# First block's mixer: band matmuls for the pooled means, token-major HGRN output, full-width projection chunks

## The reference

```python
u_pool, q_pre, f_pre, i_in, og, gates = split(h @ w_in)      # 512, 512, 512, 512, 512, 2048 columns
# pool branch: 4 groups of 128 columns, windows 2, 4, 8, 16
pooled[t] = mean of u_pool over the last min(t+1, w) tokens
pool_out  = ((pooled - u_pool) @ pool_w[group]) * pool_scale
# HGRN branch: 4 heads of 128; f_pre gives a decay per token, k = (1-lb)*sigmoid(-f_pre), q = silu(q_pre)
o = hgrn2_chunkwise(q, k, v=i_in, log_f)                     # decayed causal linear attention
o = o * rsqrt(mean(o*o over the head's 128 columns) + 1e-6) * hgrn_norm
hgrn_out = o * silu(og)
merged = sigmoid(g0) * (pool_out @ w_pool_proj) + sigmoid(g1) * (hgrn_out @ w_hgrn_proj)
return merged @ w_out
```

## Time and profile before

| | |
|---|---|
| median of 3 runs | 2721.94 us |
| the profiled execution | 2722.93 us, span 2720.9 us, mean granted TensorE clock 0.974 |
| busy in the span | TensorE 95%, VectorE 57%, ScalarE 46%, GpSimd 4% |
| DMA | 453.30 MB, 167 GB/s on average |
| first mixer call | z chunks start at 228.60 us, w_out goes on at 388.69 us |
| second mixer call | z chunks start at 807.11 us, w_out goes on at 975.98 us |

### The profile page before, as it was taken

One profiled execution on the slowest core, in us unless ns is written; L12 is line 12 of the kernel. 1 busy time (PEld: TensorE's weight loads), 2 busy tenths in 40 slices (PEclk: granted clock), 3 DMA queues, 4 the chain that ended last, 5 costly groups with the idle time before them and its releaser, 6 DMA issues.

```text
span 2720.9 us, 33264 instructions
## 1 busy us (share of the span) xinstructions
PE 2572.2 (95%) x14040; PEld 2216.7 (81%) x14040; DVE 1541.2 (57%) x1557; ACT 1246.6 (46%) x1336; POOL 100.3 (4%) x154
## 2 busy tenths in 40 slices
PE   7999889999998889999998899899999998999998
PEld 6889878888888878887888788788888887798787
DVE  5556855555467765464556436655554665365654
ACT  4436534434446444444443665444343434744442
POOL 0001300000001200000000010000000000100000
PEclk9999989999999999999999899999999988999999
DMA  7545135455443345465543225454554432253552
GB/s 271 186 163 208 68 133 212 172 203 201 170 174 140 109 143 213 170 230 184 197 180 117 87 103 206 153 210 170 190 211 174 178 131 93 98 197 139 203 180 96
DMA packets 69571, 453.30 MB, mean 167 GB/s; under 512 B 7808, under 2 KB 9984, under 8 KB 19632
## 3 DMA queue, kind: packets, MB, share of 16 engines
q1 hardware_dynamic: 64080, 432.22, 43.9%
...
## 4 chain that ended last, share of the span: by engine, by line
PE 82%; DVE 8%; ACT 6%; issue 4%; DMA 0%; POOL 0%; DVEq 0%; SPq 0%; ACTq 0%; POOLq 0%
PE acc L508 20%; PE acc L510 20%; PE acc L509 20%; PE acc L476 5%; PE acc L478 5%; PE acc L477 5%; ACT w_hi L409 3%; DVE w_lo L413 2%; PE aux L577 1%; PE aux L670 0%; PE stat L524 0%; PE bc L524 0%; DMA raw<-in_w 0%; PE aux L944 0%; DVE tmp L1624 0%
## 5 line engine op out<-in xcount | busy, mean ns | idle before, releaser
L413 DVE TENSOR_TENSOR w_lo<-raw,w_hi 128x2048 fp32r<-128x2048 f32 (+1 forms) x438 | 944.6, 2159 | 827.0 <-ACT w_hi L409 825.0
L409 ACT ACTIVATE w_hi<-raw 128x2048 fp32r<-128x2048 f32 (+1 forms) x438 | 787.6, 1802 | 657.4 <-PE acc L510 580.1
L508 PE MATMUL acc<-w_hi,x_hi 128*128 128x512 f32 (+1 forms) x1632 | 641.6, 393 | 31.3 <-DVE x_lo L1699 19.7
L510 PE MATMUL acc<-w_lo,x_hi 128*128 128x512 f32 (+1 forms) x1632 | 635.2, 389 | 0.0
L509 PE MATMUL acc<-w_hi,x_lo 128*128 128x512 f32 (+1 forms) x1632 | 634.9, 389 | 0.0
L508 PEld LDWEIGHTS acc<-w_hi,x_hi 128*128 128x128 f32 x1632 | 308.9, 189 | 98.6 <-issue 25.2
L476 PE MATMUL acc<-x_hi,w_hi 128*128 128x256 f32 x1280 | 371.2, 290 | 5.3 <-DVE w_lo L413 5.3
L477 PE MATMUL acc<-x_lo,w_hi 128*128 128x256 f32 x1280 | 366.2, 286 | 0.0
L478 PE MATMUL acc<-x_hi,w_lo 128*128 128x256 f32 x1280 | 366.0, 286 | 0.0
L510 PEld LDWEIGHTS acc<-w_lo,x_hi 128*128 128x128 f32 x1632 | 308.6, 189 | 63.9
L509 PEld LDWEIGHTS acc<-w_hi,x_lo 128*128 128x128 f32 x1632 | 308.9, 189 | 61.2
...
## 6 DMA issues: line engine op xcount, KB each, us to landing
...
```

What stands on the lines that cost most here:

```text
L409: nc.scalar.activation(w_hi[:, slot, 0:kind], raw[:, slot, 0:kind], ACT.Copy).then_inc(hi_done, 1)
L413: nc.vector.tensor_tensor(w_lo[:, slot, 0:kind], raw[:, slot, 0:kind], w_hi[:, slot, 0:kind].bitcast(F32), ALU.subtract).then_inc(lo_done, 1)
L508: nc.tensor.matmul(out, vh, wh, start=first and k == 0, stop=False)
L510: last = nc.tensor.matmul(out, vh, wl, start=False, stop=last_k and k == nk - 1)
```

## The change

- **Pooled means.** u is no longer transposed and summed. TensorE multiplies the token-major u by a constant band matrix per group, which gives (mean - u) channel-major in one step: 144 columns from the first 128 tokens, 128 from the second. ScalarE copies the result out, and the pool matrices follow one chunk later. GpSimd's sums and VectorE's block of means are gone; the constants (`mixc`, 128 x 1600) are loaded on GpSimd's queue behind `pool_w`.
- **Forget gates.** ScalarE and VectorE do each step for both halves of z before the next step, behind the splits of chunks 8 and 9.
- **Order of the units.** Unit 0 waits for k and q only. The nine iterations now run with chunks 8 to 16 (output gate twice, token-major over both chunks; then seven gate chunks), and chunk 17 follows unit 17. Two output-gate steps of VectorE stand in iteration 1, the pool branch's low parts in iteration 2.
- **HGRN output.** It is computed token-major. ScalarE squares each head with the sum as a second output and takes the root, VectorE multiplies by inverse root and output gate in one step, TensorE transposes the product, and ScalarE and VectorE split it. Statistics matmuls and broadcast are gone.
- **Projections.** Their weights come as four wide chunks instead of eight half ones (26 chunks per mixer instead of 30). `proj` runs half a chunk into one bank, so the order of the matmuls stays.
- **Merge.** VectorE has one split between the four merge steps instead of one behind each.

```diff
-MIX1 = [WIDE] * 18 + [HALF] * 8 + [WIDE] * 4
+MIX1 = [WIDE] * 26
...
+def mixer_constants(i):
+
+
+    s, t = np.arange(2 * P)[:, None], np.arange(2 * P)[None, :]
+    bands = []
+    for w in WINDOWS:
+        m = ((s <= t) & (s > t - w)) / np.minimum(t + 1, w) - (s == t)
+        bands += [m[:P, :BAND], m[P:, P:]]
+    bands = np.concatenate(bands, 1).astype(np.float32)
+    gain = [np.broadcast_to(i["hgrn_norm"][l], (P, 512)) for l in range(LAYERS)]
+    return np.ascontiguousarray(np.stack([np.concatenate([bands, g], 1) for g in gain]))
...
-                turn_block(UT, lambda p: pe.wait_ge(u_rows, 2 * (l + 1)), l, u_turned)
-                for j in range(5, 10):
+                pe.wait_ge(mixc_loaded, 16 * (l + 1))
+                pe.wait_ge(u_rows, 2 * (l + 1))
+                for g in range(4):
+                    band, cols = MIXC[:, g * BANDS:(g + 1) * BANDS], slice(g * P, (g + 1) * P)
+                    out = flips[g // 2][:, (g % 2) * S:(g % 2 + 1) * S]
+                    nc.tensor.matmul(out[:, 0:BAND], UT[:, 0, cols], band[:, 0:BAND], start=True, stop=False,
+                                     skip_group_check=True)
+                    last = nc.tensor.matmul(out[:, P:S], UT[:, 1, cols], band[:, BAND:BANDS], start=False, stop=True,
+                                            skip_group_check=True)
+                    if g % 2:
+                        last.then_inc(pooled_done, 1)
+                two_tiles(c0 + 5, t0 + 5, 8, x_hi, x_lo)
+                for g in range(4):
+                    if g % 2 == 0:
+                        pe.wait_ge(pooled_ready, 2 * l + g // 2 + 1)
+                    last = nc.tensor.matmul(flips[g // 2][:, (g % 2) * S:(g % 2 + 1) * S], pool_w[:, g * P:(g + 1) * P],
+                                            PD[:, g], start=True, stop=True)
+                    if g % 2:
+                        last.then_inc(pool_mixed, 1)
+                for j in range(6, 8):
...
-                            pe.wait_ge(forget_ready, 1 + 2 * l + 1)
-                            pe.wait_ge(pool_parts, 4 * (l + 1))
+                            pe.wait_ge(k_ready, 2 * (l + 1))
+                            pe.wait_ge(q_ready, 2 * (l + 1))
...
+                def proj(c, tile, a, src_hi, src_lo, wait_k):
+
+                    if a == 0:
+                        chunk_ready(c)
+                    bank_free(tile)
+                    for tl in range(2):
+                        for k in range(4):
+                            if tl == 0 and a == 0:
+                                wait_k(k)
+                            last = mm3(ps(tile)[:, tl * S:(tl + 1) * S], *wblock(c % RING, 8 * a + 4 * tl + k),
+                                       src_hi[:, k], src_lo[:, k], k == 0, k == 3)
+                    last.then_inc(chunk_done if a else tile_done, 1)
...
+                for j in range(9):
+                    if j < 2:
+                        both(c0 + 8 + j, t0 + 8, j)
+                    else:
+                        two_tiles(c0 + 8 + j, t0 + 8 + j, 8, x_hi, x_lo)
                     unit(2 * j)
                     unit(2 * j + 1)
-                unit(16)
-                unit(17)
-                two_tiles(c0 + 18, t0 + 18, 4, br_hi, br_lo)
+                two_tiles(c0 + 17, t0 + 17, 8, x_hi, x_lo)
...
-                two_tiles(c0 + 19, t0 + 19, 4, br_hi, br_lo)
-                pe.wait_ge(o_sq, 2 * (l + 1))
...
-                last.then_inc(o_stat, 1)
...
+                for tt in range(2):
+                    for h in range(HEADS1):
+                        out = aux[:, tt, h * P:(h + 1) * P]
+                        rows = lambda b: flat(V[:, 2 * b:2 * b + 2])[:, h * P:(h + 1) * P]
+                        last = nc.tensor.matmul(out, A[:, h, tt * P:(tt + 1) * P], rows(tt), start=True, stop=tt == 0)
+                        if tt:
+                            last = nc.tensor.matmul(out, A2[:, h // 2, (h % 2) * P:(h % 2 + 1) * P], rows(0),
+                                                    start=False, stop=True)
+                    last.then_inc(o_done, 1)
+
...
+                        proj(c0 + 18 + p, t0 + 18 + 2 * p + a, a, br_hi, br_lo, pool_part)
+                        if p and a == 0:
+                            pe.wait_ge(ho_ready, 2 * (l + 1))
+                            for q in range(2):
+                                for h in (2 * q, 2 * q + 1):
+                                    for tt in range(2):
+                                        at = (h % 2) * S + tt * P
+                                        last = nc.tensor.transpose(flips[q][:, at:at + P], HO[:, tt, h * P:(h + 1) * P],
+                                                                   ident[:, :])
+                                last.then_inc(ho_turned, 1)
+                for p in range(2):
+                    for a in range(2):
+                        proj(c0 + 20 + p, t0 + 22 + 2 * p + a, a, br_hi[:, 4:8], br_lo[:, 4:8], ho_part)
...
+                    if p == 0:
+                        for q in range(2):
+                            act.wait_ge(pooled_done, 2 * l + q + 1)
+                            nc.scalar.activation(flat(PD[:, 2 * q:2 * q + 2]), flips[q][:, :], ACT.Copy).then_inc(pooled_ready, 1)
+                    ahead.to(c + 4)
+                ac.settle()
+                for p in range(2):
                     nc.scalar.activation(FL[:, 2 * p:2 * p + 2], FL[:, 2 * p:2 * p + 2], ACT.Ln, bias=1.0).then_inc(f_ln, 1)
-                    if p == 0:
-                        turned_u()
-                    emptied(act, tile)
-                    nc.scalar.activation(K[:, 2 * p:2 * p + 2], FA[:, 2 * p:2 * p + 2], ACT.Exp, scale=-1.0).then_inc(k_exp, 1)
-                    if l:
+                for p in range(2):
+                    act.wait_ge(fa_ready, 2 * l + p + 1)
+                    nc.scalar.activation(K[:, 2 * p:2 * p + 2], FA[:, 2 * p:2 * p + 2], ACT.Exp, scale=-1.0)\
+                        .then_inc(k_exp if l else k_ready, 1)
...
+                        gate(j - 2)
...
+                gate(7)
+                choose_sqrt()
+                for tt in range(2):
+                    act.wait_ge(o_done, 2 * l + tt + 1)
+                    for h in range(HEADS1):
+                        at = 8 + 4 * tt + h
+                        ac(nc.scalar.activation(JUNK1[:, 0:P], aux[:, tt, h * P:(h + 1) * P], ACT.Square,
+                                                accum_out=small[:, at:at + 1]))
+                        ac.settle()
+                    nc.scalar.activation(small[:, 16 + 4 * tt:20 + 4 * tt], small[:, 8 + 4 * tt:12 + 4 * tt], ACT.Sqrt,
+                                         scale=4.0 / P, bias=eps_col[:, 2:3]).then_inc(o_sd, 1)
                 ahead.to(c0 + 18 + 4)
                 for p in range(2):
-                    act.wait_ge(o_done, 2 * l + p + 1)
-                    nc.scalar.activation(flat(QT[:, 2 * p:2 * p + 2]), aux[:, p, :], ACT.Square).then_inc(o_sq, 1)
+                    act.wait_ge(ho_turned, 2 * l + p + 1)
+                    nc.scalar.activation(flat(br_hi[:, 4 + 2 * p:6 + 2 * p]), flips[p][:, :], ACT.Copy).then_inc(ho_hi, 1)
...
+                def out_gate(tt):
+                    tile = t0 + 8 + tt
+                    dve.wait_ge(qog_tanh, 4 * l + tt + 3)
+                    vc(V_.scalar_tensor_tensor(OGT[:, tt], OGTANH[:, tt], 1.0, ps(tile), ALU.add, ALU.mult))
+                    vc.settle()
+                    dve.sem_inc(acc_taken[tile % RING], 1)
+                    dve.wait_ge(mixc_loaded, 16 * (l + 1))
+                    V_.tensor_tensor(OGT[:, tt], OGT[:, tt], HG, ALU.mult).then_inc(og_ready, 1)
...
+                    if j == 1:
+                        out_gate(0)
+                        out_gate(1)
+                    if j == 2:
+                        pool_low()
+                    ahead.to(c0 + 8 + j + 4)
...
+                dve.wait_ge(og_ready, 2 * (l + 1))
+                for tt in range(2):
+                    dve.wait_ge(o_sd, 2 * l + tt + 1)
+                    rs = small[:, 8 + 4 * tt:12 + 4 * tt]
+                    vc(V_.reciprocal(rs, small[:, 16 + 4 * tt:20 + 4 * tt]))
+                    vc.settle()
+                    for h in range(HEADS1):
+                        cols = slice(h * P, (h + 1) * P)
+                        ins = V_.scalar_tensor_tensor(HO[:, tt, cols], aux[:, tt, cols], rs[:, h:h + 1], OGT[:, tt, cols],
+                                                      ALU.mult, ALU.mult)
+                        if h == HEADS1 - 1:
+                            ins.then_inc(ho_ready, 1)
+                        else:
+                            vc(ins)
+                vc.settle()
                 pool_gate(0)
+                pool_gate(1)
+                ahead.to(c0 + 18 + 4)
                 for p in range(2):
-                    dve.wait_ge(o_done, 2 * l + p + 1)
...
+                    dve.wait_ge(ho_hi, 2 * l + p + 1)
```

(16 more changed lines are left out.)

293 lines of the change are left out of this document (114 added, 179 removed).

## The result

The changed kernel takes 2689.27 us (median of 4 runs, 2687.6 to 2693.84) against 2722.78 of before beside it on the same chip (2720.96 to 2723.83): ratio 0.9881, 95% interval 0.9869 to 0.9894. The forecast was 2689.0. The profiled execution took 2687.6 us, its span is 2685.9, 35.0 less than before.

What follows compares the result with a forecast made beforehand. TensorE (82% of the chain) and its waits bound the kernel. Calls of 143.0 and 148.2 us save 37.8; after slow-clock charges the gain is 33, from 2722.9 to 2690, as median 2689 us; range 2677 to 2704.

Steps and rivals of the forecast that it cites:

- Step 1: From the first forget-gate chunk to the end of units 0 and 1: 34.1 us in call one, 36.5 in call two.
- Step 2: Unit iterations 1 and 2: 8.9 and 11.1 us in call one, 11.6 and 11.2 in call two.
- Step 3: Iterations 3 to 8 through the last gate chunk: 55.1 us per call, no idle time before units 16 and 17.
- Slow clock: Charge for slow chunks behind pairs of waits up to iteration 2: 1.3 us in call one, 3.5 in call two.
- The rival of a slow clock in every iteration: In all 18 unit iterations a wait slows the chunk behind it, 2.9 us each: 2736 us; chance 0.04.
- Step 4: Output matmuls, projections, transposes, first w_out matmuls: 29.1 us per call; HGRN low parts at 14.9, asked for at 15.0.
- The rival of a late output chain: Squares and sums take twice 0.5 us, low parts come 4 us late, merge wait stays near 9: 2698; chance 0.17.
- Step 5: At the merge, four steps with one split between them: wait of 4.7 us per call in place of 9.2.
- Iterations free of VectorE: Unit iterations take the 7.54 us of half splits and iterations 1 and 2 settle at 8.4: 2675 us; chance 0.09.
- the ring: In each unit iteration, the closed loop of steps over VectorE and ScalarE, 8.37 us; the prediction called it four engines.
- That the change doesn't do what it says: The bands come late and the pool branch waits as before: 2 x 5 us back, 2699 us; chance 0.05.

Runs made afterwards that it cites:

- z_by_half: Changed kernel with the forget gate's steps on ScalarE and VectorE done one half of the heads after the other: 2694.32 us.
- pool_wait: Changed kernel with the pool branch's low parts ahead of the units on VectorE, and unit 0 waiting for them: 2696.25 us.
- Gates_spread: Changed kernel with VectorE's output gates moved to iterations 2 and 3 and the pool branch's low parts to 4 and 5: 2682.52 us.
- out_late: Changed kernel with each head's output squared twice on ScalarE, 16 squares where there were 8: 2691.9 us.
- Half_proj: Changed kernel with the projection weights as eight half chunks again, a split behind each merge step: 2693.7 us.
- split_last: Changed kernel with VectorE's split of the first w_out chunk behind the fourth merge step, not between third and fourth: 2679.49 us.

## Why the prediction was right, step by step

| step | predicted, call one / two | measured |
|---|---|---|
| 1, to units 0 and 1 | 34.1 / 36.5 | 33.8 / 36.7 |
| 2, iteration 1 | 8.9 / 11.6 | 8.9 / 12.5 |
| 2, iteration 2 | 11.1 / 11.2 | 12.1 / 10.4 |
| 3, through the last gate chunk | 55.1 / 55.1 | 57.1 / 56.4 |
| 4, output and projections | 29.1 / 29.1 | 29.5 / 29.5 |
| 5, merge wait | 4.7 / 4.7 | 4.6 / 4.6 |
| slow clock, apart | 1.3 / 3.5 | 2.5 / 1.6, in the steps above |
| sum | 144.3 / 151.7 | 145.9 / 150.1 |

The two sums are both 296.0. That is luck in part: call one came out 1.6 over, call two 1.6 under, and a wait of 1.8 us in each call that the prediction says is not there is made up for by terms that came out smaller.

**Step 1** held. No wait at the bands or the pool matrices, no wait for unit 0 in call one, 2.7 us for q in call two where 2.5 was counted through. z_by_half and pool_wait show that this count was the thing to do: each piece put in front of q or behind it comes out on TensorE one for one in call two, and not at all (or 1.0) in call one.

**Step 2** held within 1 us. Gates_spread shows that VectorE's gates are the reason for its length. At full clock iteration 2 of call one takes 11.2 us (pool_wait) where 11.1 was counted; the 0.8 to 12.1 is the low clock. In call two the low clock is in both iterations, 0.8 and 0.8, so without it they take 11.7 and 9.6: the first as counted (11.6), the second 1.6 less than the 11.2, since TensorE, delayed, finds its first unit ready.

**Step 3** failed in one line: "no idle before units 16 and 17". There are 1.8 us in each call, for GpSimd. GpSimd's and VectorE's timelines in the change:

```profile
331.83 1.78 POOL L2017 TENSOR_TENSOR tmp<-tmp 128x512 f32<-128x512 f32 x1 [5.19 <-ACT tmp L1186]
```

```profile
331.79 0.69 DVE L1691 TENSOR_TENSOR tmp<-tmp 128x512 f32<-128x512 f32 x1
```

I wrote "queries ready", and they nearly are: unit 16 is through at 332.0 and unit 17's queries are done at 332.5. Its keys take GpSimd 1.78 us from the same exponentials and are done at 333.6. I had followed one of the two operands, though the wait for the other stood in the trace of before (the 1.9 us above). The other excess, 1.7 us in call one, is the slow chunk at 282.93 (7.55 us instead of 5.83). Units 16 and 17 themselves took 1.0 instead of 1.4, and the pair of units and the chunk that follow the slow chunk had no wait and took 7.5 instead of 8.4; that gives 1.3 back.

**Slow clock.** The mechanism is there in both calls, behind a pair of waits as charged, and the sizes were the wrong way round: 1.3 was charged in call one and 2.5 was spent, 3.5 in call two and 1.6 spent, 4.1 in place of 4.8. How much the low clock takes is not to be had from the waits: pool_wait has the same pair of waits in iteration 2 at 1.00. The 1.9 that call two did not spend, and the 1.6 less of its iteration 2, covered the wait that step 3 had missed. The rival of a slow clock in every iteration is out: 8.37 us at 1.00 (the row of 300.50), with 0.6 us idle in each. The prediction cited the Trainium skill ("TensorE: Matmul & The Clock Gate", "HAM oscillation — how this bites in real kernels") for it; the trace agrees with it only where waits are longer, and the waits of the page's own loop are about 3 to 5 us.

**Step 4**'s length is right within 0.4 us, and its margin was not "bare": a square with its read takes 0.40 us from start to start, not 0.5,

```profile
344.43 0.28 ACT L1205 ACTIVATE tmp<-aux 128x128 f32<-128x128 f32 x1
344.60 0.19 ACT L1205 ACTIVATION_READ_ACCUMULATOR tmp<-aux 128x1 f32 x1
344.83 0.28 ACT L1205 ACTIVATE tmp<-aux 128x128 f32<-128x128 f32 x1
```

and out_late had to add 3.2 us to cost 1.1. The rival of a late output chain, to which I gave 0.17, was never near.

**Step 5** held: one split between four merge steps, 4.58 us. Half_proj puts the splits back and gets 9.3, split_last takes the last one out and gets 1.2.

**The other rivals.** Iterations free of VectorE: they stayed at 8.37 as forecast, and the ring shows why. A half split takes some 2 us out of it, half of 2.21 and of 1.94, which puts it under TensorE's own work: the 7.54 of the earlier trace rows. That the change doesn't do what it says: TensorE has no wait at the bands or the pool matrices in either call, and pool_wait costs only what stands behind q on VectorE.

**Where the 33 us in the calls came from**, by the undone parts: the place of the last gate chunk 16.2, full projection chunks 5.6, the forget gate's order 3.3 (2.6 of it table loads), the pool branch's wait 2.0, which is 27.1 one by one and 28.5 together. The first two depend on each other, so these are shares only in the changed kernel. The 4.5 left are TensorE's own work by argument, not by a run: nothing undoes the HGRN output or the bands alone. The prediction had the same list in waits but not in these shares: it named the stretch at units 16 and 17 (8.26 us with 3.5 of work) without a price of its own.
